# The copies of mixer B's states, issued in the projection stage

## The reference

```
xn = RMSNorm(x);  q, k, v of mixer A and of mixer B = split(xn @ w_in)     # 3072 columns
h  = x + W_out [ A(xn) ; B(xn) ]          # A: differential attention, B: dilated sliding window
y  = h + PEER(RMSNorm(h))                 # 8 heads, 16 of 16384 experts per head
k_ext = jnp.concatenate([state_b_k[l], kb], axis=1)      # samples: 2048 rows and 4 new ones
v_ext = jnp.concatenate([state_b_v[l], vb], axis=1)
bks.append(k_ext[:, -n_buf:])             # the last 2048 rows are outputs
bvs.append(v_ext[:, -n_buf:])
```

## Time and profile before

| | |
|---|---|
| median of 3 runs | 3925.64 us (3924.53 to 3928.91) |
| the profiled execution | 3928.74 us |
| its span, first to last instruction | 3927.2 us |
| busy: PE, DVE, ACT, POOL | 3241.9, 2798.5, 1213.3, 1220.6 us |
| read from HBM, written | 911.56 MB, 146.44 MB |
| q0 (GpSimd), q1 (SP) | 595.57 MB, 385.63 MB |

### The profile page before, as it was taken

How to read it: one execution, slowest core, us unless ns; L and a number is a source line. 1 busy time by engine, 2 the same in 40 slices (tenths; PEclk the granted TensorE clock), 3 DMA queues, 4 the chain that set the end, 5 groups by cost and what they waited for, 6 DMA issues and landing times. The chain is left out here.

```text
span 3927.2 us, 63929 instructions
## 1 busy us (share of the span) xinstructions
PE 3241.9 (83%) x22587; PEld 2878.6 (73%) x22587; DVE 2798.5 (71%) x6620; ACT 1213.3 (31%) x2349; POOL 1220.6 (31%) x1219
## 2 busy tenths in 40 slices
PE   7997769666646777764755999999999999999998
PEld 5776547523323555553655999999999999999998
DVE  6562644211102488889854999999999999999998
ACT  5442435312202232225972222222222222222221
POOL 0000000024432000000003556565756555555554
PEclk9998989877867888887987999999999999999999
DMA  4323122299978432323999999999999999999997
GB/s 140 113 73 95 56 64 66 101 357 387 387 263 312 145 108 96 125 70 101 330 303 335 340 331 345 346 343 332 351 352 334 335 345 356 336 335 344 347 334 281
DMA packets 405587, 992.67 MB, mean 253 GB/s; under 512 B 38002, under 2 KB 165972, under 8 KB 404116
## 3 DMA queue, kind: packets, MB, share of 16 engines
q0 software_dynamic: 150048, 595.57, 41.6%
q1 hardware_dynamic: 253140, 385.63, 28.2%
q10 hardware_dynamic: 2224, 9.44, 0.6%
HBM read 911.56 MB, written 146.44 MB: 269 GB/s over the span
## 5 line engine op out<-in xcount | busy, mean ns | idle before, releaser
L1852 PE MATMUL banks<-x_hi,u_hi 128*128 128x320 f32 x2048 | 634.1, 310 | 62.6 <-DVE x_lo L1942 62.6
L1865 PE MATMUL banks<-coef_hi,v_hi 128*128 128x320 f32 x2048 | 633.8, 309 | 6.1 <-issue 6.1
L1852 PE MATMUL banks<-x_hi,u_lo 128*128 128x320 f32 x2048 | 633.8, 309 | 0.0
L1852 PE MATMUL banks<-x_lo,u_hi 128*128 128x320 f32 x2048 | 633.8, 309 | 0.0
L1865 PE MATMUL banks<-coef_lo,v_hi 128*128 128x320 f32 x2048 | 633.6, 309 | 0.0
L1865 PE MATMUL banks<-coef_hi,v_lo 128*128 128x320 f32 x2048 | 633.6, 309 | 0.0
L1813 POOL DMA_INDIRECT uv_row<-in_v_rows,expert_tok x384 | 478.8, 1247 | 382.5 <-DVE y_tok L1996 328.0
L1813 POOL DMA_INDIRECT uv_row<-in_u_rows,expert_tok x384 | 462.1, 1203 | 358.5 <-DVE dots L1970 308.4
L1996 DVE SCALAR_TENSOR_TENSOR y_tok<-uv_row,share,y_tok 128x1024 f32<-128x1024 f32 x415 | 530.3, 1278 | 0.7
L1970 DVE CUSTOM_DVE_ANT_0 uv_row<-uv_row,x_tok 128x1024 f32<-128x1024 f32 x416 | 506.4, 1219 | 0.0
L1852 PEld LDWEIGHTS banks<-x_hi,u_hi 128*128 128x128 f32 x2048 | 385.4, 188 | 62.8 <-DVE x_lo L1942 62.8
(11 more groups left out here) (267 smaller groups left out, 5519.5 us busy)
## 6 DMA issues: line engine op xcount, KB each, us to landing
keys_sa<-in_cache_k SPq DMA_DIRECT2D x256, 256.0 KB
values_sa<-in_cache_v POOLq DMA_DIRECT2D x256, 256.0 KB, 6.7
uv_raw<-in_u SPq DMA_DIRECT2D x128, 512.0 KB
uv_raw<-in_v SPq DMA_DIRECT2D x128, 512.0 KB
scratch_gates<-stage SPq DMA_DIRECT2D x10, 4096.0 KB, 29.9
gates<-scratch_gates SPq DMA_DIRECT2D x128, 320.0 KB
out_win_k_out<-in_state_k POOLq DMA_DIRECT2D x8, 4088.0 KB
out_win_v_out<-in_state_v POOLq DMA_DIRECT2D x8, 4088.0 KB
```

What stands on the lines that cost most here:

```text
L1852: ins = nc.tensor.matmul(bank[:, 2 * r + c, 0:CH], u[r][a][:, k * P:(k + 1) * P], x2[b][:, k, c * CH:(c + 1) * CH], start=(k == 0 and a == b),
L1865: ins = nc.tensor.matmul(bank[:, 4 + n % 4, 0:CH], v[j][a][:, k * P:(k + 1) * P], coef[j][b][:, c * CH:(c + 1) * CH], start=(j == 0 and a ...
```

## The change

All sixteen copies of old rows are issued by GpSimd in the projection stage, behind the loads of x. Copy n waits for `w_lo` to reach 2 + n * 10 // 16 (integer division), which gives 2, 2, 3, 3, 4, 5, 5, 6, 7, 7, 8, 8, 9, 10, 10, 11. GpSimd leaves the stage when all sixteen have landed. The new rows of all samples become one transfer for the keys and one for the values, at the start of routing, without a wait. The spreading stage has nothing left on GpSimd.

```diff
--- before.py
+++ after.py
@@ -123,6 +123,7 @@
         xT_in_psum, xn_ready = sems("xT_in_psum"), sems("xn_ready")
         x_hi, x_lo = sems("x_hi_ready"), sems("x_lo_ready")
         made = sems("products_made")
+        state_kept = sems("state_kept")
         squared = sems("h_squared")
         h_ready = sems("h_ready")
         hss_ready, hstd_ready = sems("hss1_ready"), sems("hstd1_ready")
@@ -223,6 +224,10 @@
             for t in range(TILES):
                 since(pool, xs_ready, t - 1)
                 pool.dma_start(x_rows[t % 2][:, :], io["x"][t * P:(t + 1) * P, :]).then_inc(x_loaded[t % 2], 16)
+            for n in range(2 * DB):
+                pool.wait_ge(w_lo, 2 + n * 10 // (2 * DB))
+                keep_state(pool, io, n // DB, n % DB, state_kept)
+            pool.wait_ge(state_kept, 32 * DB)
 
         @block.tensor
         def _(pe):
@@ -1053,13 +1058,18 @@
 LAST = PAIRS - HALFK
 
 
-def move_state(pool, io, which, b, moved):
-
-    state, out, new = (io[name] for name in (("state_k", "win_k_out", "kb"), ("state_v", "win_v_out", "vb"))[which])
+def keep_state(pool, io, which, b, moved):
+
+    state, out = (io[name] for name in (("state_k", "win_k_out"), ("state_v", "win_v_out"))[which])
     kept = (STATE - DQ) * SEG
     src, dst = state[b, :, :].rearrange("s c -> (s c)"), out[b, :, :].rearrange("s c -> (s c)")
     pool.dma_start(dst[0:kept].rearrange("(a c) -> a c", a=64), src[DQ * SEG:].rearrange("(a c) -> a c", a=64)).then_inc(moved, 16)
-    pool.dma_start(out[b, STATE - DQ:, :], new[SEQ + b * DQ:SEQ + (b + 1) * DQ, :]).then_inc(moved, 16)
+
+
+def add_to_state(pool, io, which, moved):
+
+    out, new = (io[name] for name in (("win_k_out", "kb"), ("win_v_out", "vb"))[which])
+    pool.dma_start(out[:, STATE - DQ:, :], new[SEQ:NT, :].rearrange("(b q) c -> b q c", q=DQ)).then_inc(moved, 16)
 
 
 def load_route_weights(act, io, weights, loaded):
@@ -1216,11 +1226,9 @@
 
         @block.gpsimd
         def _(pool):
-            if tiles[0] == 0:
-                for b in range(DB):
-                    pool.wait_ge(h_ready, b + 1)
-                    move_state(pool, io, 0, b, state_moved)
-                pool.wait_ge(state_moved, 32 * DB)
+            for which in range(2):
+                add_to_state(pool, io, which, state_moved)
+            pool.wait_ge(state_moved, 32)
 
         @block.tensor
         def _(pe):
@@ -1522,7 +1530,6 @@
         apart = sb("apart_squared", [P, 2, BY_ACT, P])
         neg_ready, apart_ready, act_gated = sems("neg_i2_ready"), sems("apart_ready"), sems("act_gated")
         iota_loaded = sems("iota5_loaded")
-        state_moved = sems("state_v_moved")
         places_ready = sems("places_ready")
         gated_ready = sems("gated_ready")
         rows_used = sems("rows_used")
@@ -1562,13 +1569,6 @@
                     ins = nc.vector.tensor_scalar(row2[g % RING][:, j, :], iota[:, :], picksT[:, 1, tok], picksT[:, 2, tok],
                                                   ALU.is_equal, ALU.mult)
                 ins.then_inc(gated_ready, 1)
-
-        @block.gpsimd
-        def _(pool):
-            for b in range(DB):
-                since(pool, staged, b * (GROUPS // DB))
-                move_state(pool, io, 1, b, state_moved)
-            pool.wait_ge(state_moved, 32 * DB)
 
         @block.tensor
         def _(pe):
```

## The result

| | before | with the change |
|---|---|---|
| median | 3926.06 us (3924.53 to 3928.91, 5 runs) | 4063.93 us (4060.61 to 4066.33, 5 runs) |
| span of the profiled execution | 3927.2 us | 4059.1 us |
| ratio to before | | 1.0349, 95% interval 1.0337 to 1.0360 |

What follows compares the result with a forecast made beforehand. PE was taken to pace projection, where bunched copies starve SP's stores: -9 us (spreading) and +132 us (stalls) on 3928.74 us give 4052, or 4049 us by the median; range 4005 to 4085 for 8 in 10.

Steps and rivals of the forecast that it cites:

- Bound and place: PE sets the pace in projection, VectorE in routing; sixteen copies stall projection, while removing eight copies from routing gives 0.
- What is taken away: Spreading stage: ScalarE's two waits for gate stores held up by copies, 9.0 us, go away; -9 us.
- One record of each queue in turn: DMA engines: beside a 65 KB copy, SP's queue advances one record per engine in 2.7 to 3.3 us, whatever its size.
- The first rival: Projection stage: SP moves several records per 65 KB record, so no stall is left, only -9; 3917 us, chance 0.06.
- The stalls: Projection stage, first five segments: bunched copies starve SP's stores, so engines wait for buffer slots; +132 us, range 115 to 152.
- the 12 us of a copy: Projection stage: time taken for each copy in a bunch, chosen between 10.9 and 13.3 us, by the undisturbed copy's 11.7.
- the same 5 us: Stall formula in projection: 2 us until the copies start plus 3 us for the rest of the store and its landing.
- The 2.7 us of the lower bound: DMA engines: time per record from 47 and 47 records in 8 us; four make the 10.9 us copy.
- Restarts: Projection stage: PE's half clock after four stands, up to 4 us each, 16 in all, against work finished meanwhile; taken as 0.
- Weights late next: Projection stage: SP's weight loads starve too, landing some 10 us after a bunch, but over 20 us of cover is left.
- Half the stalls: Rival, projection stage: only half of the 132 us appears; 3983 us, counting +10 to +80; chance 0.13.
- slow copies: Rival, projection stage: copies in line exceed 13.3 us, or weights come late; at 15 us a copy +45, 4094 us; chance 0.07.

## Why the prediction was right, step by step

- **Bound and place.** Right: routing and experts don't move, and the projection stage pays. GpSimd's own wait at the end of that stage cost nothing.
- **What is taken away, -9 us.** Right: 9.0 us in the profile, and the run without copies is 9 us faster than before (ratio 0.9977).
- **One record of each queue in turn.** Right, and the step on which all hung. It was read from copies beside gate stores, and held beside stores of qk_T (67 and 67), beside stores of v and weights (60 and 59 from 238 to 248 us), with records of 8 KB (394 and 394), and in routing (994 and 994). The first rival, that SP keeps up, is refuted with it. The rows also disagree with the packet rule of the Trainium skill (DMA: Bandwidth & Descriptors, section Queues, rings and completion order), by which a turn is typically 9 to 17 descriptors. The prediction took that rule for SP's queue alone. It is stated for every queue, so equal counts over 10 us do not by themselves speak against it; the 15 single pairs from 100 to 103 us do.
- **The stalls.** The places were right, all five, and the sum was 132 us where the change added 141.8: 47, 25, 41, 19, 0 forecast, 49.0, 26.9, 45.3, 19.9, 0.7 measured. The mis-sized term is the 12 us of a copy. From the end of the split, or of the last load of x, to the end of the wait, less the same 5 us, the first four segments give 12.4, 12.7, 13.2 and 12.4 us; the third is (290.19 - 232.54 - 5) / 4. That is between the 12 that I chose and the upper bound of 13.3.
- **Where the 12 came from.** The copy of the earlier trace rows was not undisturbed: in that window SP's queue moved 1851 records. And 73.2% of 16 us is the mean of 16 engines; from the start of its first record to the end of its last the copy took 12.4 us. The shares of the earlier trace rows give 3.0 us a record (90.6% of 160 us over 48) and 3.1 us (114.2% of 128 us, which is 8 us on 16 engines, over 47), so 12.1 and 12.4 us for four. The 2.7 us of the lower bound left out that records ran on beyond the window. Why a copy in line takes up to 13.2 us is not shown. That SP's records run beside it does not explain it: before the change one copy of values had the engines to itself, from 1844 to 1859 us. 80.4% of 15 us is 12.1 us, and from its first record to its last it took 13.3. Queue q1 moved nothing in that window, q0 this:

```profile
q0 software_dynamic: 112, 4.19, 80.4%
```

- **Restarts.** Taken as 0 and nearly so: the stage grew by 142.5 us, 0.7 more than the waits. The half clock cost PE 8.7 us of busy time, within the 16 forecast. PE's idle time grew by 134.3 us against 141.8 of added waits, so PE worked on for some 7.5 us while another engine already stood; the forecast had up to 5 us for each stall.
- **Weights late next.** Right that they are not: they land up to 54.8 us after their issue, yet no wait of the changed kernel names them beyond the 6.8 us at the very start, where no copy runs.
- **Half the stalls, or slow copies.** Neither came. By the sums above the copies in line took 12.4 to 13.2 us, within the forecast's bounds.

What stays open: how small a record must be for the projection stage to carry the copies without a wait, and what the weights in SP's queue add to the waits.

## What to carry to other kernels

Before moving a large transfer under a stage with idle DMA engines, look at the record counts of both queues in a window where they overlap, not at the DMA share: here a queue with 65 KB records left the other one record per 3 us. Then compare the length of the bunch, not of the whole, with the time for which the other queue's next store is covered: two copies per 52 us tile cost nothing, sixteen at once cost 163 us in the same stage. If a bunch can't be avoided, smaller records shorten the turn: 4064 us with 65 KB and 4023 with 8 KB, and 3973 with 4 KB, where two copies also left later.

## What the runs showed of the hardware

Pieces of a copy that follow each other in memory don't stay pieces: 496 pieces of 8 KB went out as records of 63 KB and 2032 of 2 KB as records of 65 KB. Rows of 2 KB taken at a stride of sixteen rows still went out at 3.9 KB a record on the mean. So the size of a record must be read from the trace (MB over records), not from the access pattern.
